# The time-step tile of a Mamba-2 layer as 4-byte products in four column strips

## The reference

```python
def rmsnorm(x, w):
    y = xf * lax.rsqrt(jnp.mean(xf * xf, axis=-1, keepdims=True) + EPS)
    return (y * w.astype(jnp.float32)).astype(x.dtype)

def mamba2_mixer(u, conv_state, ssm_state, w_in, ...):
    proj = u @ w_in                       # (tokens, 1024) @ (1024, 5152)
    z, xbc, dt = jnp.split(proj, [D_INNER, D_INNER + CONV_DIM], axis=-1)
    ...
    xbc_act = jax.nn.silu(conv + conv_b)  # depthwise convolution of 4 taps over xbc
    ...
    dtf = jax.nn.softplus(dt.astype(jnp.float32) + dt_bias.astype(jnp.float32))
    A = -jnp.exp(a_log.astype(jnp.float32))
    y, final = ssd_chunked(...)           # uses the running sum of dtf * A
```

## Time and profile before

| | us |
|---|---|
| median of 3 runs | 1008.78 |
| lowest and highest run | 1008.69, 1009.45 |
| span of the profiled execution | 1008.4 |
| TensorE busy in it | 974.3 (97%) |
| VectorE busy | 580.3 (58%) |
| ScalarE busy | 469.5 (47%) |
| GpSimd busy | 363.7 (36%) |

### The profile page before, as it was taken

How to read it: one execution, slowest core, us unless ns; L and a number is a source line. 1 busy time by engine, 2 the same in 40 slices (tenths; PEclk the granted TensorE clock), 3 DMA queues, 4 the chain that set the end, 5 groups by cost and what they waited for, 6 DMA issues and landing times.

```text
span 1008.4 us, 18539 instructions
## 1 busy us (share of the span) xinstructions
PE 974.3 (97%) x7372; PEld 896.8 (89%) x7372; DVE 580.3 (58%) x1433; ACT 469.5 (47%) x819; POOL 363.7 (36%) x275
## 2 busy tenths in 40 slices
PE   9999999999999999999998999999999999999988
PEld 8998999889998999879988789997899888997877
DVE  4225431444224421356687779957798577886872
ACT  6435713463235612467355455244552545526453
POOL 2331234134231143116442445425344253543600
PEclk9999999999999999999999999999999999999989
DMA  6522223322223222102425624256341662426203
GB/s 201 194 67 83 65 85 112 103 83 84 84 70 144 84 84 90 44 21 61 131 88 151 188 71 124 73 159 180 87 137 45 170 178 77 137 64 211 76 11 100
DMA packets 144117, 106.35 MB, mean 105 GB/s; under 512 B 10258, under 2 KB 135364, under 8 KB 143840
## 3 DMA queue, kind: packets, MB, share of 16 engines
q1 hardware_dynamic: 117208, 92.25, 29.5%
q10 hardware_dynamic: 26824, 12.93, 4.8%
HBM read 92.44 MB, written 16.79 MB: 108 GB/s over the span
## 4 chain that ended last, share of the span: by engine, by line
PE 83%; DVE 10%; issue 3%; ACT 1%; POOL 1%; DMA 0%; ACTq 0%; SPq 0%; DVEq 0%; POOLq 0%
PE pp L1211 20%; PE pp L1213 19%; PE pp L1212 19%; PE pS L1327 3%; PE pS L1551 2%; DVE cv L1923 2%; PE pT_ L1530 1%; PE pO L1540 1%; PE pO L1544 1%; PE pO L1373 1%; PE pO L1372 1%; PE pO L1491 1%; POOL w_lo_raw L621 1%; PE pS L1463 1%; DVE z L2065 1%
## 5 line engine op out<-in xcount | busy, mean ns | idle before, releaser
L621 POOL TENSOR_TENSOR w_lo_buf<-w_raw_buf,w_hi_buf 128x512 fp32r<-128x512 f32 x214 | 287.4, 1374 | 485.4 <-ACT w_hi_buf L702 247.6
L1211 PE MATMUL pp<-h_hi,w_hi_buf 128*128 128x280 f32 (+1 forms) x1248 | 378.1, 303 | 5.2 <-DVE rb L1897 2.8
L1213 PE MATMUL pp<-h_hi,w_lo_buf 128*128 128x280 f32 (+1 forms) x1248 | 362.9, 291 | 0.0
L1212 PE MATMUL pp<-h_lo,w_hi_buf 128*128 128x280 f32 (+1 forms) x1248 | 362.2, 290 | 0.0
L1211 PEld LDWEIGHTS pp<-h_hi,w_hi_buf 128*128 128x128 f32 x1248 | 235.2, 188 | 16.0 <-issue 8.0
L1212 PEld LDWEIGHTS pp<-h_lo,w_hi_buf 128*128 128x128 f32 x1248 | 235.2, 188 | 4.6 <-issue 4.1
L1213 PEld LDWEIGHTS pp<-h_hi,w_lo_buf 128*128 128x128 f32 x1248 | 235.2, 188 | 0.0
L702 ACT ACTIVATE w_hi_buf<-w_raw_buf 128x2048 fp32r<-128x2048 f32 (+1 forms) x55 | 104.0, 1892 | 23.4 <-DMA w_raw_buf<-in_w_ssm_in 16.4
L1709 DVE TENSOR_TENSOR x<-x,pp 128x272 f32<-128x272 f32 (+3 forms) x128 | 56.4, 440 | 79.5 <-PE pp L1213 78.7
L1211 PE MATMUL pp<-og_hi,w_hi_buf 128*128 128x280 f32 (+2 forms) x256 | 75.5, 295 | 1.7 <-DVE og_lo L1830 1.1
L1213 PE MATMUL pp<-og_hi,w_lo_buf 128*128 128x280 f32 (+2 forms) x256 | 74.5, 291 | 0.0
(11 more groups left out here) (338 smaller groups left out, 1724.1 us busy)
## 6 DMA issues: line engine op xcount, KB each, us to landing
w_raw_buf<-in_w_attn_in SPq DMA_DIRECT2D x16, 1024.0 KB, 5.2
w_raw_buf<-in_w_ssm_in SPq DMA_DIRECT2D x16, 1024.0 KB, 5.4
w_raw_buf<-in_w_attn_out SPq DMA_DIRECT2D x8, 1024.0 KB, 5.0
s_in<-in_state_ssm SPq DMA_DIRECT2D x32, 256.0 KB, 4.2
out<-s_in SPq DMA_DIRECT2D x32, 256.0 KB, 3.2
seg<-a_scratch ACTq DMA_DIRECT2D x16, 512.0 KB, 4.5
w_raw_buf<-in_w_ssm_out SPq DMA_DIRECT2D x8, 1024.0 KB, 5.6
w_raw_buf<-in_w_attn_in SPq DMA_DIRECT2D x8, 512.0 KB, 6.3
```

Of the source, the lines that this page charges most:

```text
L621: ins = pool.tensor_tensor(low_buf(n)[:, piece], raw[n % RAW_SLOTS][:, piece], high_buf(n)[:, piece].bitcast(F32), ALU.subtract)
L1211: pe.matmul(dst, hi[:, k, cols], a_hi[:, k, tk], start=(k == 0), stop=False)
L1212: pe.matmul(dst, hi[:, k, cols], a_lo[:, k, tk], start=False, stop=False)
L1213: mm = pe.matmul(dst, lo[:, k, cols], a_hi[:, k, tk], start=False, stop=(k == depth - 1))
```

## The change

The time-step tile no longer uses the split into high and low parts. Its slab is 32 columns wide for each k. ScalarE multiplies the raw weights of blocks 0 to 3 by the norm's weight of their features, GpSimd those of blocks 4 to 7, into `w_steps` [128, 8, 32]. TensorE multiplies these four-byte weights with x itself, not with h: for each half and each k one matmul of 32 weight columns, into partitions 32(k % 4) to 32(k % 4) + 31 of the PSUM tensor pS. Each strip of 32 partitions so holds the sum over two blocks k. VectorE adds the four strips: two copies out of PSUM, two additions with PSUM, one of the two results; then it multiplies by rs. The bc tile takes over the waits for h_ready that the time-step tile had.

```diff
-            return [(0, 32, at(5120, 32)), (32, 96, at(5024, 96))]
+            return [(0, N_DT, at(5120, N_DT))]
...
+                    if slabs[n][0] == "dt":
+                        src, by = slab_view(raw[n % RAW_SLOTS], "dt"), norm_all(1)
+                        pool.tensor_tensor(w_steps[:, STRIPS:KM, :], src[:, STRIPS:KM, :],
+                                           by[:, STRIPS:KM].unsqueeze(2).to_broadcast([P, KM - STRIPS, N_DT]),
+                                           ALU.mult).then_inc(w_lo, 1)
...
+                    if slabs[n][0] == "dt":
+                        src = slab_view(raw[n % RAW_SLOTS], "dt")
+                        for k in range(STRIPS):
+                            ins = act.activation(w_steps[:, k, :], src[:, k, :], ACT.Copy, scale=norm_c(1, k))
+                        ins.then_inc(w_hi, 1)
...
-                    elif (kind, s) == ("dt", GROUPS) and half == 0:
+                    elif (kind, s, tile, half) == ("bc", GROUPS, 0, 0):
                         pe.wait_ge(h_ready, KM + k + 1)
...
+            def project_steps():
+
+                n = slab_no[("dt", GROUPS, 0)]
+                pe.wait_ge(w_hi, n + 1)
+                pe.wait_ge(w_lo, n + 1)
+                pe.wait_ge(soft_a, UNITS * GROUPS)
+                for half in range(2):
+                    tk = span("dt", GROUPS, half)
+                    for k in range(KM):
+                        if half == 0:
+                            pe.wait_ge(p_evac, tile_done("out", GROUPS - 1, k))
+                        r = N_DT * (k % STRIPS)
+                        mm = pe.matmul(pS[r:r + N_DT, half, 0:HALF], w_steps[:, k, :], x[:, k, tk],
+                                       start=(k < STRIPS), stop=(k >= STRIPS))
+                    mm.then_inc(p_done, 1)
...
-            project("dt", GROUPS, 0, 0)
-            project("dt", GROUPS, 0, 1)
+            project_steps()
             sum_x()
...
             dve.wait_ge(s_late, 64)
             dve.wait_ge(p_done, tile_done("dt", GROUPS, 0))
+            strips = [pS[N_DT * i:N_DT * (i + 1), :, 0:HALF] for i in range(STRIPS)]
+            by_half = lambda t: t.rearrange("p (h t) -> p h t", h=2)
+            dve.tensor_copy(by_half(t1[:, :]), strips[0])
+            link(dve.tensor_copy(by_half(t2[:, :]), strips[1]))
+            dve.tensor_tensor(by_half(t1[:, :]), by_half(t1[:, :]), strips[2], ALU.add)
+            link(dve.tensor_tensor(by_half(t2[:, :]), by_half(t2[:, :]), strips[3], ALU.add))
+            link(dve.tensor_tensor(t1[:, :], t1[:, :], t2[:, :], ALU.add))
             for half in range(2):
                 tk = slice(half * HALF, (half + 1) * HALF)
-                dve.tensor_tensor(t1[:, tk], bank("dt", GROUPS, 0, half)[0:32], rs[0:32, tk],
-                                  ALU.mult).then_inc(p_evac, 1)
+                dve.tensor_tensor(t1[:, tk], t1[:, tk], rs[0:N_DT, tk], ALU.mult).then_inc(p_evac, 1)
```

More of the change, by code:

```diff
@@ L213, in slab_view @@
     def slab_view(buf, kind):
[L214 removed]
+        k, c = {"out": (4, 512), "dt": (8, N_DT)}.get(kind, (8, 256))
         return buf[:, 0:k * c].rearrange("p (k c) -> p k c", k=k)
```

19 lines of the change are left out of this document (11 added, 8 removed).

## The result

The changed kernel takes 1015.5 us (median of 5 runs, 1011.73 to 1017.68), the kernel before, beside it, 1008.81 (5 runs, 1008.69 to 1009.8): a ratio of 1.006 [1.0043, 1.0077]. The forecast was 1010.6 us, with a range to 1012.9. The direction was right, the size was not. The profiled execution took 1015.77 us, with a span of 1014.0; before's span was 1008.4.

A forecast was written before the change was run, and what follows sets the result against it. It took TensorE to bound the kernel up to the first tile after the time-step transposes, VectorE from 506.72 us on. 3.15 - 2.0 + 0.65 = 1.8 us late, so 1008.8 + 1.8 = 1010.6 us; range 1008.6 to 1012.9.

The forecast's parts named there:

- what is given back: Third x tile on VectorE: 2.0 us lost beside GpSimd come back, less 0.65 for what the shift newly costs.
- the clock: Rival, chance 0.27: clock falls to half speed after TensorE's two pauses, 0.9 to 4 us on top, 1012.4 us.
- TensorE's time, pause, no gain from it: Time-step tile: strips take 1.9 us, then a pause of about 3.8 before sum_x; bc tile gains 0.1 at most.
- VectorE's sum: Behind the wait for rs: five added instructions, 3.64 us together, make the time-step sum 3.7 us late.
- TensorE waits for the bank: Before the second bc tile: first bc evacuation late, so TensorE stands still and its following tiles end 3.15 us later.
- 0 to 0.7 us is left: Second x tile: taps slowed beside GpSimd, mostly covered by VectorE's former 1.89 us wait; 0 to 0.7 us remain.
- GpSimd's start near 504.8: GpSimd's slab split beside the x tiles: start set by a weight load issued behind rs, so it stays near 504.8.
- The rival's lower prices: Clock fall: 0.9 us on sum_x, and 1.7 for half a stretch at half speed after the second pause.
- nothing later makes it up: After 512.56 us: VectorE's gapless chain releases all that follows, so the 1.8 us delay carries to the end.

The follow-up runs named there:

- e7: Changed kernel with the four strips copied out by ScalarE and added by TensorE instead of VectorE, which multiplies out of PSUM; 1011.53 us.
- e10: e2 without GpSimd's low part of the third and fourth x tiles' weight slab, a one-column copy in its place; 1009.72 us.
- e11: Kernel before without GpSimd's low part of the third and fourth x tiles' weight slab, a one-column copy in its place; 1009.17 us.
- e2: Changed kernel with idle products in TensorE's two pauses, four before sum_x and three before the second bc tile; 1011.31 us.
- e1: Changed kernel with VectorE's five strip instructions moved ahead of its wait for rs; 1013.07 us.
- e6: Changed kernel with VectorE's evacuation of the first bc half moved ahead of its wait for ScalarE's Exp; 1012.03 us.
- e8: e7 with VectorE's evacuation of the first bc half moved ahead of its wait for ScalarE's Exp; 1010.19 us.
- e9: e8 with three idle products in TensorE's pauses, one before the strip sum and two before sum_x; 1010.78 us.
- e13: e12 with VectorE's product with the exponential moved behind the first x tile's first evacuation; 1009.41 us.
- e3: Changed kernel with the strip sum ahead of VectorE's wait for rs and four idle products before sum_x; 1014.85 us.
- e12: e8 with the first bc half's 16 products that need no low part moved into TensorE's pause before the strip sum; 1011.18 us.

## Why the prediction was wrong

Two steps of the prediction failed, what is given back and the clock; the clock, which the sum had at nothing, weighs more.

- **TensorE's time, pause, no gain from it: right.** 2.2 us for the strips (forecast 1.9), pause 3.48 (3.8), and the bc tile no earlier: it starts 1.23 us after xsum in both kernels.
- **VectorE's sum: right.** Forecast five instructions of 0.73 us and 3.7 us late; the first evacuation is 3.66 later after xsum, and e7, which takes the five away, gets 3.0 of it back. The Trainium skill, page "TensorEngine Tiling (Array Packing)", section "PSUM Bottleneck", warned that emptying PSUM may become the bottleneck; the trace agrees: 4 us less on TensorE, 3.7 more on VectorE.
- **TensorE waits for the bank: right.** Forecast 3.15 us late. The second bc tile's first product comes 3.25 us later after xsum (11.28 for 8.03), and at the fourth tile it is 3.24 without collision and with the clock held (e10 against e11). TensorE stood still for only 1.60 of it; for the rest the clock had stretched the tile ahead.
- **"What is given back": wrong, by 0.9 us.** I had 2.0 back less 0.65 (the middle of two parts of 0 to 0.7 is 0.7, which changes little), so 1.35. Measured: before loses 2.0 to GpSimd and e2's form 1.5, so 0.5. The third tile did get its 2.0 back. The failed step is the second tile's "0 to 0.7 us is left": it lost 3.5 us and not 1.9 to 2.6. The taps lost 1.8, no more than forecast; the copy and the product, which I had left out, lost 1.7, and 1.9 was all the wait could cover. GpSimd's start near 504.8 was luck: in e2 it came at 504.92, released not by a weight load but by TensorE's bc tiles, and in the changed kernel itself it moved with them to 506.52, since the slow clock had delayed them.
- **The clock: the rival I left out of the sum.** This is the other failed step, and with 1.55 us in this stretch (after against e2) the larger term. I had set pauses of 3.8 and 3.15 us against one of 4.02, taken them for shorter and left the fall out of the sum; it came behind both, and e7 shows one behind far less. The rival's lower prices were right: half a stretch at half speed, which I had at 1.7, for the second pause, and the 0.9 on sum_x, which the changed kernel's profile does not show but e1, e6, e7 and e8 do (sum_x 2.0 to 2.24 us instead of 1.2). The first fall stretched the first bc tile and was hidden by the wait for the bank, the second is paid.

The sum, with its measured terms: 3.24 for the bank, 1.53 - 2.01 for the collision, 1.55 for the clock: 4.3 us. That this is what the table has (30.79 - 26.48) is no test, since the terms are the distances from row to row of it (after, e2, e10, e11, before). Forecast were 1.8. With 4.3 the total would be 1013.1 us, just outside the range; without the clock it would have been 2.8, so 1011.6 us, inside it.

The rest of the 6.7 us between the medians is not in that stretch. In the profiled executions, 1.0 us lies at the start and 0.3 behind the fifth tile, together with the 4.3 the 5.6 us between the spans. Another 1.1 us is the choice of before's profiled execution: every run that lists both took at least 1.76 us longer than its span, and not 0.4, so this one, with a span of 1008.4, took some 1010.2 and was itself slower than its kernel's median.

Every run lists its mean granted clock (to 0.001, so what follows is rough), and over the 19 groups of runs (15 kernels, and before beside them) 0.001 less clock goes with 0.75 us more within a group (least squares). The changed kernel's runs have 0.9934 on average, before's 0.9956 to 0.9962: some 1.9 us, and the falls in the stretch are in that. Taken to a clock of 1, before is at 1006.2 to 1006.9 us, the changed kernel at 1010.0 (standard error 0.6), e2 at 1009.0, e8 at 1007.4, e9 at 1008.2 and e13 at 1007.2 (0.3 to 0.4 each): roughly what the table says for the changed kernel and e2. For e9 and e13 it doesn't: they are 0.3 and 1.1 us ahead at the fifth tile and yet not faster in total. In e13's profiled execution 1.5 us went at 450 to 462 us, ahead of every edited instruction. Stretches of e13_high_first_dt, columns as above:

```profile
427.00:450.00 23.00, 22.83 (x133) 18.30 (x132) 12.78 (x63) 15.10 (x37) 5.03 (x4) 1.00 0.04 7
450.00:455.00 5.00, 3.37 (x18) 3.16 (x19) 3.38 (x10) 4.99 (x14) 0.00 (x0) 0.78 0.00 0
455.00:462.00 7.00, 7.00 (x44) 6.04 (x42) 2.98 (x8) 2.79 (x8) 0.00 (x0) 0.91 0.00 0
```

e1, e3 and e12 are late there by the same 1.5 us, and the other twelve executions have 1.00. Yet TensorE pauses there alike in all (1.10 or 1.11 us before the product at 452.73 here), so the same pause is followed by a fall in some executions and not in others. Whether that comes with these kernels or by chance, the runs don't settle.

Nor does the end of the stretch settle the total. Behind the fifth tile's evacuation the profiled executions take 486.8 us in before, 484.5 in e2, 483.7 in e3 and 487.8 in e11, with three, one, one and four falls of the clock on the way. So "nothing later makes it up" does not hold for single executions, and the totals of e10 and e11 differ by 0.0012, 1.2 us, where the stretch has 3.2, just outside what their intervals allow. How much of such differences is the kernels' stays open.
